# Score groups of two items side by side on TensorE, with four score banks, one value bank and a ring of three projection banks, in a dilated-attention encoder layer

## What is computed

```python
hn = rmsnorm(x, norm_g)
q, k, v, z_a, hc, gb, gc, z_b, g = split(hn @ w_in)      # 3 x 1536, 512, 4 x 512, 2048
for gi, dil in enumerate((1, 4, 16)):                    # 8 heads of 64 in each group
    # each query sees keys at 0, +-dil, ..., +-64 * dil
    s = q . k / 8 - slope * distance;  p = exp(s);  den_gi = sum(p);  o_gi = p @ v
attn = sum_gi(o_gi) / sum_gi(den_gi)                     # after log-sum-exp weighting
a = (silu(z_a) * attn) @ w_attn_out
c = (silu(z_b) * gb * conv3(gc * hc)) @ w_conv_out
y = rmsnorm(x + (sigmoid(g_a) * a + sigmoid(g_c) * c) @ w_o, final_g)
```

## Time and profile before

| | us |
|---|---|
| time before, median of 3 runs | 1541.97 |
| lowest, highest of the 3 | 1538.83, 1619.25 |
| the profiled execution | 1538.82 |
| its span on the slowest core | 1537.3 |
| PE busy in the span | 1487.3 (97%) |
| DVE busy | 940.9 (61%) |
| ACT busy | 703.1 (46%) |

### The profile page before, as it was taken

The page is one execution under the profiler, slowest core; times in us unless marked ns, Lnnn a source line. Parts: engine busy times, 40 slices in busy tenths (PEclk is TensorE's granted clock), DMA queues, the critical chain, the costliest instruction groups (busy, mean ns, idle before and its releaser), DMA issues.

```text
span 1537.3 us, 28178 instructions; the slowest of 8 cores (1533.4 to 1537.3 us)
## 1 busy us (share of the span) xinstructions
PE 1487.3 (97%) x11208; PEld 839.4 (55%) x11360; DVE 940.9 (61%) x1476; ACT 703.1 (46%) x1170; POOL 142.8 (9%) x287
## 2 busy tenths in 40 slices
PE   4999999999999999999999999999999999999997
PEld 2454445576566565666866664666444444444443
DVE  4677777235765857567558575685854444444445
ACT  4445544334574656645356557565422222222222
POOL 4212222000010000000000000001100000000001
PEclk9999999999999999999999999999999999999999
DMA  9874545313151422403315205143943222233133
GB/s 244 156 129 101 114 100 88 60 42 79 36 97 15 99 53 52 65 15 64 93 32 102 29 22 105 26 92 50 179 123 110 83 94 98 83 110 108 58 110 124
DMA packets 67764, 132.07 MB, mean 86 GB/s; under 512 B 8752, under 2 KB 34480, under 8 KB 67376
## 3 DMA queue, kind: packets, MB, share of 16 engines
q1 hardware_dynamic: 49296, 96.70, 22.3%
q0 software_dynamic: 18336, 33.56, 15.9%
HBM read 130.17 MB, written 33.62 MB: 107 GB/s over the span
## 4 chain that ended last, share of the span: by engine, by line
PE 85%; DVE 7%; DMA 3%; ACT 2%; issue 2%; SPq 0%; POOL 0%; DVEq 0%; POOLq 0%; ACTq 0%
PE ps L403 49%; PE ps L696 8%; PE ps L1078 7%; PE ps L1108 7%; PE ps L847 5%; PE ps L716 4%; PE ps L807 3%; DVE X L897 2%; DMA X<-w_co 2%; PE ps L448 1%; ACT X L393 1%; DMA gc_s<-X 1%; DVE X L821 1%; DMA X<-xw 1%; ACT X L817 1%
## 5 line engine op out<-in xcount | busy, mean ns | idle before, releaser
L403 PE MATMUL ps<-hnT,wbf 128*128 128x512 bf16 (+1 forms) x2904 | 651.3, 374 | 10.7 <-issue 3.2
L403 PEld LDWEIGHTS ps<-hnT,wbf 128*128 128x128 bf16 x3008 | 281.2, 98 | 313.8 <-issue 8.4
L393 ACT ACTIVATE X<-ps 128x512 bf16<-128x512 f32 (+2 forms) x320 | 219.0, 694 | 206.4 <-PE ps L403 198.2
L821 DVE TENSOR_TENSOR X<-X,et 128x512 bf16<-128x512 bf16 x384 | 159.0, 422 | 217.2 <-ACT X L817 207.9
L817 ACT ACTIVATE X<-ps 128x512 bf16<-128x512 f32 x384 | 207.8, 596 | 148.7 <-PE ps L807 142.6
L403 PE MATMUL ps<-hnT,X 128*128 128x512 bf16 (+1 forms) x1126 | 243.3, 367 | 1.4
L1083 DVE SCALAR_TENSOR_TENSOR hnT<-hnT,ps 128x512 f32<-128x512 f32 x128 | 87.1, 685 | 147.0 <-PE ps L1078 147.0
L403 PEld LDWEIGHTS ps<-hnT,X 128*128 128x128 bf16 x1152 | 107.9, 98 | 125.4 <-DMA X<-w_in 0.4
L696 PE MATMUL ps<-wbf,hnT 128*128 128x128 bf16 x2720 | 164.7, 220 | 0.0
L696 PEld LDWEIGHTS ps<-wbf,hnT 128*128 128x128 bf16 x2720 | 158.5, 114 | 0.2
L978 ACT ACTIVATE hnT<-ps,cf 128x512 f32<-128x512 f32 x128 | 87.4, 683 | 140.4 <-PE ps L403 124.5
(11 more groups left out here) (61 smaller groups left out, 994.8 us busy)
## 6 DMA issues: line engine op xcount, KB each, us to landing
X<-xw SPq DMA_DIRECT2D x80, 512.0 KB, 5.6
wbf<-w_in POOLq DMA_DIRECT2D x95, 256.0 KB, 5.9
y<-X SPq DMA_DIRECT2D x31, 512.0 KB, 2.9
X<-w_in POOLq DMA_DIRECT2D x17, 256.0 KB, 21.0
ga_s<-X SPq DMA_DIRECT2D x32, 128.0 KB, 3.0
X<-ga_s SPq DMA_DIRECT2D x8, 512.0 KB, 6.5
X<-gc_s SPq DMA_DIRECT2D x8, 512.0 KB, 7.0
gc_s<-X SPq DMA_DIRECT2D x24, 128.0 KB, 5.7
```

Source lines behind the costliest of these rows:

```text
L393: return op("act", lambda e: e.activation(out=out, in_=in_, func=AF.Copy), reads=reads, writes=writes)
L403: fns.append(lambda e, kt=kt: e.matmul(bv.cols(c0, n), lhsT=wf(kt), rhs=hnT.cols(kt * WT + t0, n), start=(kt == 0), stop=(kt == 7)))
L821: op("dve", lambda e, hh=hh, eoff=eoff: e.tensor_tensor(out=prv.ap(hh * 512, [[256, 2], [1, 256]]), in0=prv.ap(hh * 512, [[256, 2], [1, 25 ...
```

## The change

- Score groups go in pairs: an even item emits its own score group and that of the next item directly behind it. The two use banks 2, 3 and 4, 5 (`sb_`).
- `stage_a` is split: scores (`stage_a`), exponentials (`stage_e`), masks (`stage_m`). The exponentials of the odd item are emitted in the even one, behind its value group and masks.
- The value group lags by two items instead of one, over the borders of units (`pend` in place of `prev_b`). It comes before the masks of the item that emits it.
- All value groups use bank 6. The ring of projection banks is 0, 1, 7.
- `start_piece` is listed behind the four Q pieces, since value groups of the unit before last still read that set of buffers in items 0 and 1.
- Finalization parts are queued when the value group of an odd item is emitted, thus one item later. In the last unit the weights and `load_chunk(0)` are issued in item 1, and the last gate piece is held back to stand between the last two value groups.

```diff
-        pb_ring = {"r": (0, 1, 4, 5)}
+        pb_ring = {"r": (0, 1, 7)}
...
-            pieces.append((0, start_piece))
...
                 pieces.append((512, qpiece))
+            pieces.append((0, start_piece))
...
-                    def stage_a(quad=quad, j=j, st=st):
+                    sb_ = 2 + 2 * (len(items) % 2)
+
+                    def stage_a(quad=quad, j=j, st=st, sb_=sb_):
                         pslot = prc["i"] % 3
                         prc["i"] += 1
                         st["pslot"] = pslot
-                        prv = pr_[pslot].v
-                        sb_ = 2
...
+                    def stage_e(st=st, sb_=sb_):
+                        pslot = st["pslot"]
+                        prv = pr_[pslot].v
                         for hh in range(2):
-                            bv = bank(sb_ + hh)
+                            op("act", lambda e, bv=bank(sb_ + hh), hh=hh: e.activation(
+                                out=prv.cols(hh * 512, 512), in_=bv.cols(0, 512), func=AF.Exp, scale=0.125),
+                               reads=[R_bank[sb_ + hh]], writes=xg(65536 + 2048 * pslot + 1024 * hh, 1024))
+
+                    def stage_m(st=st):
...
-                        ob = 6 + (obank["i"] % 2)
-                        obank["i"] += 1
+                        ob = 6
...
-                    items.append((stage_a, stage_b))
+                    items.append((stage_a, stage_e, stage_m, stage_b))
...
-            def do_b(ib):
-                items[ib][1]()
-                if g == 0 and ib % 2 == 1 and ib < nit - 1:
+            def do_b(ib, items=items, g=g, hp=hp, h=h):
+                items[ib][3]()
+                if g == 0 and ib % 2 == 1:
                     fin_add(hp, h, ib // 2)
 
             for i in range(nit):
-                items[i][0]()
+                if i % 2 == 0:
+                    items[i][0]()
+                    items[i + 1][0]()
+                    items[i][1]()
+                if len(pend) > 1:
+                    pend.pop(0)()
+                items[i][2]()
+                if i % 2 == 0:
+                    items[i + 1][1]()
+                pend.append(lambda ib=i, do_b=do_b: do_b(ib))
                 fin_run()
-                if i == 0 and prev_b[0] is not None:
-                    prev_b[0]()
-                    prev_b[0] = None
-                    if last_unit:
-                        c_weights_1()
-                        c_weights_2(range(3))
-                        load_chunk(0)
-                if i >= 1:
-                    do_b(i - 1)
+                if last_unit and i == 1:
+                    c_weights_1()
+                    c_weights_2(range(3))
+                    load_chunk(0)
                 while pi < len(nxt) and (i == nit - 1 or spent < total * (i + 1) / nit):
+                    assert i > 0 or nxt[pi][0] == 512
+                    if last_unit and pi + 1 == len(nxt):
+                        break
                     spent += nxt[pi][0]
                     nxt[pi][1]()
                     pi += 1
                 gi[0] += 1
...
-        prev_b[0]()
+        pend.pop(0)()
+        nxt[-1][1]()
+        pend.pop(0)()
```

More of the change, by code:

```diff
@@ L764, in proj_pieces @@
             return pieces
-        obank = {"i": 0}
         prc = {"i": 0}
@@ L813, in stage_a @@
                         pe_group(fns, reads=kres + qt.r, writes=[R_bank[sb_], R_bank[sb_ + 1]])
+                    def stage_e(st=st, sb_=sb_):
+                        pslot = st["pslot"]
+                        prv = pr_[pslot].v
                         for hh in range(2):
-                            bv = bank(sb_ + hh)
+                            op("act", lambda e, bv=bank(sb_ + hh), hh=hh: e.activation(
+                                out=prv.cols(hh * 512, 512), in_=bv.cols(0, 512), func=AF.Exp, scale=0.125),
+                               reads=[R_bank[sb_ + hh]], writes=xg(65536 + 2048 * pslot + 1024 * hh, 1024))
+                    def stage_m(st=st):
+                        pslot = st["pslot"]
+                        prv = pr_[pslot].v
+                        for hh in range(2):
                             pres = xg(65536 + 2048 * pslot + 1024 * hh, 1024)
-                            op("act", lambda e, bv=bv, hh=hh: e.activation(
-                                out=prv.cols(hh * 512, 512), in_=bv.cols(0, 512), func=AF.Exp, scale=0.125),
-                               reads=[R_bank[sb_ + hh]], writes=pres)
                             eoff = es_ * 1536 + (g * 2 + hh) * 256
@@ L1003, in fin_run @@
                 fin.pop(0)[2]()
-        prev_b = [None]
+        pend = []
         nu = len(units)
```

## The result

The changed kernel takes 1521.06 us (median of four executions), against 1540.4 us for the kernel before (the three shown above and one more). The ratio is 0.9874 with a 95% interval of 0.9849 to 0.9898: 1.3% less, clear of the noise, and within the 2% that the prediction said it would stay in. The forecast was 1520. One of each four executions ran on cores that were granted a lower clock (1619.25 above, 1606.32 of the changed kernel); they are in these two medians but not in the ratio, and the other three have medians of 1538.83 and 1520.35.

What follows compares the result with a forecast made beforehand. PE's own order of work was taken to bound the kernel (busy for 97% of the span). 1538.8 - 18.1 - 2.9 + 1.4 + 1.0 = 1520.2 us, forecast as 1520, range 1512 to 1536.

Steps and rivals of the forecast that it cites:

- The pair: Attention stage: score groups in pairs save 0.197 us in each of 92 pairs, -18.1 us.
- The steps 0.09, 0.33 and 0.22: Attention: score group entry 0.09 us, 0.33 until the next group starts, 0.22 for a second one streaming behind.
- it can't save more than 0.20: Upper bound on the gain of a pair of score groups, in us, since the columns have to be streamed.
- argument of 600 ns: Within a score group, serial loads and matmuls would need 600 ns; it takes 330, so loads already run under matmuls.
- rival 1: The second score group doesn't stream: only 0.09 us saved a pair, 1530.0 us in all; chance 0.18.
- The old waits: Attention stage: value groups' waits for masks on VectorE disappear with a lag of two items, -2.9 us.
- The successors: New waits from one value bank and a ring of three: 0.2 us in each of seven rounds, +1.4 us.
- the timetable: VectorE's work against PE's gates in a round: bank free in time three times, 0.1 us late once.
- Rival 2: The ring of three makes PE wait 13.9 us for gate banks held by VectorE: 1541.1 us; chance 0.10.
- Q first: Start_piece moves behind four Q projections; halo loads stay hidden, their reader the next unit, some 20 us later.
- w_co: Last unit: the issue of this weight load moves by 1.6 us, its landing by 0 to 1.6; charged +1.0 us.
- the wait of 5 us: Sign of being right: PE waits about 5 us for w_co in front of line 1078.

Runs made afterwards that it cites:

- split pair: Changed kernel with the value group of an even item emitted between the two score groups instead of behind them: 1537.04 us.
- other banks: Changed kernel with value groups of items 5 and 6 of the last unit in free score banks 2 and 4: 1519.0 us.
- lag of one: Changed kernel with value groups lagging one item instead of two; pairs, one value bank and ring of three kept: 1589.26 us.
- finer K claims: Kernel with value groups lagging one item, each K projection copy now claiming only the tiles it writes, not the whole buffer: 1543.85 us.

## Why the prediction was right, and where it wasn't

- **The pair.** It was right, and in its mechanism. The steps 0.09, 0.33 and 0.22 came out as 0.55 for a pair behind one entry. The unit lengths say 0.213 a pair where 0.197 was put; of the difference 0.01 is that a value group behind a projection takes 0.44, as the earlier trace rows with 893.90 and the new odd items have it, and 0.45 behind scores. So "it can't save more than 0.20" was too tight by that. The split pair adds that the entry behind a value group is 0.11. The choice of 0.20 over 0.09 by the argument of 600 ns was right, and rival 1 is refuted by the trace. 0.09 to 0.11 us appear at each change between 64-row and 128-row groups, and none between two 64-row groups. That fits the Trainium skill, "TensorEngine Tiling (Array Packing)", Key Properties, by which a change of the tiling mode drains the engine. The Trainium skill, "TensorE: Matmul & The Clock Gate", What overlaps and what doesn't, lets a weight load overlap a running matmul only where the row group differs; by the prediction's reading of it a pair would take 0.66, an estimate, and the trace has 0.55. The rows of the weight loads add a hint. Those of a score group start at most 0.01 us ahead of its first matmul (859.68 and 859.69), those of a value group behind a projection 0.05 ahead (864.22 and 864.27):

```profile
859.68 0.45 PEld L805 LDWEIGHTS ps<-X 64*128 64x128 bf16 x16
...
864.22 0.49 PEld L852 LDWEIGHTS ps<-X 128*128 128x128 bf16 x8
```

  So at a change the load isn't started early. Whether that is what costs the 0.1 us, or itself comes of a drain, no run here separates.
- **The old waits.** -2.9 was put. The split pair says -3.8, and that it is the lag that removes them; the -3.1 of the table is what is left of it behind the next item.
- **The successors.** +1.4 was put for seven rounds, and about 0.7 came: the four units 3, 9, 15 and 21 gain 3.1 with pairs and 3.8 without. In the rounds themselves the timetable held nearly: the third projection behind the last gate, to which it gave no margin, is 0.25 us late (the one that it had 0.1 late, a round before, is in time). One of its terms was off: it used 0.74 us for a pair of score groups where the step above it has 0.42 + 0.22 = 0.64, which takes 0.1 from each margin.

```profile
821.15 3.62 PE L403 MATMUL ps<-hnT,wbf 128*128 128x512 bf16 x16
...
825.70 3.87 PE L403 MATMUL ps<-hnT,wbf 128*128 128x512 bf16 x16
```

  Both rows are 16 matmuls, and the second has a gap in it. Rival 2's mechanism is real, but in the old order: 11.3 us for the ring there, where the expectation from the hold times was 10.5 (7 x 1.5; the prediction's 13.9 was for the new order, where it didn't come). The timetable was the step that decided between the two, and the new order's own numbers bear it out. But I made the timetable only for the rounds. Unit 12 (+4.2) was not looked at, with VectorE's two evacuations for a V piece, its staging slots and the DMA engines; and in the last unit, where each item has one piece, the same count was not made either, and might have shown the 1.9 us. The two missed losses, 6.1 us on core 1, were put at nothing. Why the last unit loses them is only partly settled: other banks gave 0.6 us back, and the rest went over to the masks.
- **Q first.** "Their reader is the next unit" was wrong. The next to wait for the halo load is ScalarE's copy of a K projection in the same unit, by the claim on the whole buffer, four times for 2.6 us in all. It did not reach PE in this order; with a lag of one item it cost 45 us. I had followed who reads the data, not who names the resource.
- **w_co.** The issue did not move: 2.74 us behind the start of the last unit before (core 1: 1068.75 and 1066.01), 2.73 now (1051.96 and 1049.23). The step assumed that POOL's load waits for the last value group because it is emitted behind it. But w_ao and w_co overwrite the Q and K buffers and the first V tiles, which that group doesn't read. What did wait is `load_chunk(0)`, which takes the place of later V tiles: 1052.66, 3.4 us behind the unit's start, where it was 1.0 (1067.05 and 1066.01). So PE waits 0.85 us for the chunk on core 1 (0.3 to 1.6 on the eight cores, 0.6 in the median) instead of 0 to 2.9 for w_co (0.5 in the median; the 2.9 is the core shown in the earlier trace rows). The charge of +1.0 was for the wrong load and about nil in sum, and the wait of 5 us didn't appear. The issues, before and after, on core 1:

```profile
1067.05 0.37 SPq L163 DMA_DIRECT2D X<-ga_s  x1
1068.75 0.75 POOL L163 DMA_DIRECT2D X<-w_co  x1
...
1051.96 0.75 POOL L163 DMA_DIRECT2D X<-w_co  x1
1052.66 0.37 SPq L163 DMA_DIRECT2D X<-ga_s  x1
```

- **The sum.** -18.1 - 2.9 + 1.4 + 1.0 = -18.6 put; -20.5 - 3.8 + 0.7 + 6.1 = -17.5 in attention on core 1. That the total came out within a microsecond is luck: an under-estimated gain and two missed losses offset each other. The main term and its sign were right by themselves, and the split pair shows it.

## What to carry to other kernels

Where PE is the bound, count its changes between 64-row and 128-row groups by the starts of groups, since a busy share of 97% hides them, and put groups of one kind side by side. Banks taken for that are paid for by the in-order queues behind them: write out when each bank comes free in the new order, for every kind of unit and for the last one, not only for the busiest. A buffer claimed as a whole makes a late load everybody's wait; claim what an instruction writes.

## What was not expected of the hardware

- A 64-row group behind a 128-row group, or the other way round, costs 0.09 to 0.11 us more than behind its own kind (1.83 against 1.74 us for the projection in front of a score group, 0.56 against 0.45 behind a value group, 0.33 against 0.22 for a score group in front of another kind).
- A DMA's landing can hang on what another engine issued just before it: the same 512 KB halo load of K lands in 3.7 to 7.2 us (median 5.4, four loads on each of eight cores) in the changed kernel, and in 8.4 to 12.9 us (median 10.8) with a lag of one, where it is issued 2.2 us behind the first of five weight loads. With the finer K claims it is issued as late and takes 9.0 to 14.0. That the weight loads do it is read from this order; no run moved them alone. An issue that moves by one item of 4 us can cross such a load and cost several times that.
- A wait of PE costs more than its length once the granted clock falls: around the end of each of four waits of 8.4 to 10.4 us its mean over 10 us was 0.65 to 0.72, and the matmuls behind it took 8.3 us more in all (the lag of one, slowest core).
